# RWKV-7 chunk products on quarters of the TensorE array: 64x64 matmuls, four tiles in step

## The reference, cut to what matters

```python
def step(S, xs):
    w_t, kk_t, a_t, k_t, v_t, r_t = xs
    sa = jnp.einsum('bhvk,bhk->bhv', S, kk_t)
    S = S * w_t[:, :, None, :] - sa[..., None] * (kk_t * a_t)[:, :, None, :] + v_t[..., None] * k_t[:, :, None, :]
    y = None if r_t is None else jnp.einsum('bhvk,bhk->bhv', S, r_t)
    return S, y
```

## Time and profile before

| | |
|---|---|
| time, median of 3 runs | 4595.56 us (4587.01 to 4595.78) |
| span of the profiled execution | 4593.0 us |
| PE busy | 4060.8 us, 88% |
| DVE busy | 1998.8 us, 44% |
| POOL busy | 1020.3 us, 22% |
| ACT busy | 601.3 us, 13% |
| DMA | 211.99 MB, mean 46 GB/s |

### The profile page before, as it was taken

One profiled execution on the slowest core, in us unless ns is written; L12 is line 12 of the kernel. 1 busy time (PEld: TensorE's weight loads), 2 busy tenths in 40 slices (PEclk: granted clock), 3 DMA queues, 4 the chain that ended last, 5 costly groups with the idle time before them and its releaser, 6 DMA issues. The chain is left out here.

```text
span 4593.0 us, 57174 instructions
## 1 busy us (share of the span) xinstructions
PE 4060.8 (88%) x24068; PEld 3313.3 (72%) x24068; DVE 1998.8 (44%) x2650; ACT 601.3 (13%) x802; POOL 1020.3 (22%) x530
## 2 busy tenths in 40 slices
PE   9888879999999969977879879879869887999999
PEld 1374667888888858866858758758858866788777
DVE  0214144333433441243366566566666634434434
ACT  0211021011000020022220020020020002010010
POOL 0220232222232233211011011011011034343332
PEclk9899979999999979987979979979979987999999
DMA  8402101111011002211010010010010021111111
GB/s 314 191 19 93 37 24 36 35 40 37 28 42 37 28 28 84 74 47 40 9 40 1 6 40 1 6 40 1 4 42 1 4 78 43 42 51 46 43 53 60
DMA packets 46501, 211.99 MB, mean 46 GB/s; under 512 B 5952, under 2 KB 6976, under 8 KB 41920
## 3 DMA queue, kind: packets, MB, share of 16 engines
q1 hardware_dynamic: 42240, 191.94, 11.8%
q10 hardware_dynamic: 4032, 16.65, 0.9%
HBM read 187.73 MB, written 20.84 MB: 45 GB/s over the span
## 5 line engine op out<-in xcount | busy, mean ns | idle before, releaser
L173 PE MATMUL ps<-u_hi,w_hi 128*128 128x512 f32 (+1 forms) x2712 | 738.7, 372 | 85.8 <-DVE u_lo L404 40.8
L173 PE MATMUL ps<-u_lo,w_hi 128*128 128x512 f32 (+1 forms) x2712 | 735.7, 371 | 0.0
L173 PE MATMUL ps<-u_hi,w_lo 128*128 128x512 f32 (+1 forms) x2712 | 734.4, 370 | 0.0
L151 POOL TENSOR_TENSOR w_hi<-w_raw,zero 128x1024 fp32r<-128x1024 f32 x176 | 338.0, 1920 | 1643.1 <-PE ps L173 1430.2
L173 PEld LDWEIGHTS ps<-u_hi,w_hi 128*128 128x128 f32 x2712 | 473.7, 190 | 181.3 <-DVE u_lo L404 41.9
L173 PEld LDWEIGHTS ps<-u_lo,w_hi 128*128 128x128 f32 x2712 | 474.4, 189 | 90.3
L173 PEld LDWEIGHTS ps<-u_hi,w_lo 128*128 128x128 f32 x2712 | 473.9, 189 | 90.3
L491 DVE SCALAR_TENSOR_TENSOR ffn_cv<-ps,small,ffn_cv 128x1023 f32<-128x1023 f32 (+1 forms) x132 | 134.1, 1016 | 804.4 <-ACT ffn_cv L625 802.8
L433 DVE SCALAR_TENSOR_TENSOR h<-ps,mod,h 128x1024 f32<-128x1024 f32 (+1 forms) x288 | 282.7, 1013 | 412.8 <-PE ps L173 412.8
L154 POOL TENSOR_TENSOR w_lo<-w_raw,w_hi 128x1024 fp32r<-128x1024 f32 x176 | 425.3, 2417 | 13.8
L1743 DVE TENSOR_TENSOR rwc_x<-rwc_x,ps 128x512 f32<-128x512 f32 x360 | 247.8, 688 | 95.8 <-PE ps L1678 95.8
(11 more groups left out here) (267 smaller groups left out, 5194.7 us busy)
## 6 DMA issues: line engine op xcount, KB each, us to landing
w_raw<-in_ffn SPq DMA_DIRECT2D x132, 512.0 KB, 3.2
ada_ring<-in_ada SPq DMA_DIRECT2D x24, 2048.0 KB, 8.3
w_raw<-in_cd_in SPq DMA_DIRECT2D x20, 512.0 KB, 3.7
z_scratch<-cd_stage ACTq DMA_DIRECT2D x15, 640.0 KB, 5.1
dft_tab<-in_dft_tok SPq DMA_DIRECT2D x8, 1024.0 KB, 4.9
h<-in_x SPq DMA_DIRECT2D x8, 640.0 KB, 12.9
w_raw<-in_ab_in SPq DMA_DIRECT2D x8, 512.0 KB, 3.7
w_raw<-in_ab_out SPq DMA_DIRECT2D x8, 512.0 KB, 3.6
```

What stands on the lines that cost most here:

```text
L151: pool.tensor_tensor(K.whi[:, slot, :], K.raw[:, raw, :], K.zero[:, 0:1].to_broadcast([P, KT * P]), ALU.add).then_inc(self.hi_done, 1)
L173: mm = pe.matmul(K.ps[:, slot, c, 0:width], wt[:, s, w], x[:, k, at:at + width], start=start and n == 0, stop=stop and n == 2)
```

## The change

The two chunks of a tile are stacked on partitions, chunk 0 on 0 to 63 and chunk 1 on 64 to 127, and a unit's matrix becomes two 64x64 ones beside each other's rows: tiles M, X, XT, PX have 64 columns a unit where they had 128. Each 128x128 matmul of the levels becomes two 64x64 ones, chunk 0 on the first diagonal quarter of the array and chunk 1 on the second. In the pair, crossed and output products head and chunk choose row and column half, so that all four quarters are used in turn.

The identity is now in every plane of `R.level`, and POOL adds it to M too. M and X then carry it, so that X is not added to but replaced: DVE copies X, ACT copies XT (before, DVE added both), and DVE masks PX. The transposed start (XT) is made by POOL in two operations as before, half as wide; a third adds the identity to M, and DVE's first X waits for it (`eyed`). The two masks of stages 1 and 2 become one DVE operation over two banks, and the two copies into `rwc_tm` one.

Four tiles instead of two are in work (`NS = 4`), each with two PSUM banks, and each stage is gone through for all four before the next: groups of 4, 4 and 2 tiles. Each kind of hand-over has its own semaphores. The mask and level tables shrink to half, and so do their loads in `rwkv_prepare`.

The diff, without the removed lines of `rwkv_chunks` (they stand above) and without what only renames; the output products of Q and Y go by `both` as those of G and HP do:

```diff
-        self.mask = keep("mask", [P, 2, 2, P])
-        self.level = keep("level", [P, 6, 2, P])
+        self.mask = keep("mask", [P, 2, 2, CL])
+        self.level = keep("level", [P, 6, 2, CL])
...
+    NS = 4
...
+    SS = temp("ss", [P, NS, 2, 2, 2, 2, CL])
+    M = temp("m", [P, NS, 4, CL])
+    X = temp("x", [P, NS, 4, CL])
+    XT = temp("xt", [P, NS, 4, CL])
+    PX = temp("px", [P, NS, 4, CL])
...
+    both = [(c, hp) for hp in range(2) for c in range(2)]
+    HALF = [slice(0, 64), slice(64, 128)]
...
+    def bank(s, b):
+        return K.ps[:, s // 2, 2 * (s % 2) + b, :]
...
+    STAGES = 3 + 2 * LV + 2
+    steps = [(n, t, t % NS, t // NS) for first in range(0, TOK, NS) for n in range(STAGES)
+             for t in range(first, min(first + NS, TOK))]
         @block.gpsimd
+            for n, t, s, turn in steps:
+                if n == 2:
+                    pool.wait_ge(masked[s], turn + 1)
+                    if turn:
+                        pool.wait_ge(sq_done[s], LV * turn)
+                    xt = units(XT[:, s])
+                    pool.tensor_tensor(xt, SS[:, s, :, 0, :, 0, :], over_heads(R.level[:, 0, :, :]),
+                                       ALU.mult).then_inc(half_t[s], 1)
+                    pool.wait_ge(half_t[s], turn + 1)
+                    pool.tensor_tensor(XT[:, s], XT[:, s], K.eye2[:, :].rearrange("p (o c) -> p o c", o=1)
+                                       .to_broadcast([P, 4, CL]), ALU.add).then_inc(xt0_out[s], 1)
+                    pool.wait_ge(m_out[s], turn + 1)
+                    pool.tensor_tensor(M[:, s], M[:, s], K.eye2[:, :].rearrange("p (o c) -> p o c", o=1)
+                                       .to_broadcast([P, 4, CL]), ALU.add).then_inc(eyed[s], 1)
...
+                elif n == 1:
+                    pe.wait_ge(tm_out[s], turn + 1)
+                    for kind, src in enumerate((R.beta, R.kappa)):
+                        for d in range(2):
+                            for c, hp in both:
+                                at = kind * 256 + d * P
+                                mm = pe.matmul(bank(s, hp)[HALF[c], at:at + P], src[HALF[hp], d, toks(t, c)],
+                                               R.ar[HALF[hp], d, t, :, HALF[c]], start=True, stop=True)
+                    mm.then_inc(pairs[s], 1)
+                elif n == 2:
+                    pe.wait_ge(masked[s], turn + 1)
+                    for d in range(2):
+                        for c, hp in both:
+                            mm = pe.matmul(bank(s, hp)[HALF[c], d * CL:(d + 1) * CL], R.ar[HALF[hp], d, t, 0, HALF[c]],
+                                           R.beta[HALF[hp], d, toks(t, c)], start=True, stop=True)
+                    mm.then_inc(crossed[s], 1)
+                elif n < 3 + 2 * LV and n % 2 == 1:
+                    j = (n - 3) // 2
+                    if j == 0:
+                        pe.wait_ge(eyed[s], turn + 1)
+                        pe.wait_ge(xt0_out[s], turn + 1)
...
+                    for u in range(4):
+                        for c in range(2):
+                            mm = pe.matmul(b0[HALF[c], u * CL:(u + 1) * CL], M[HALF[c], s, u, :], XT[HALF[c], s, u, :],
+                                           start=True, stop=True)
...
+                elif n < 3 + 2 * LV:
...
+                    for u in range(4):
+                        for c in range(2):
+                            mm = pe.matmul(b1[HALF[c], u * CL:(u + 1) * CL], X[HALF[c], s, u, :], PX[HALF[c], s, u, :],
+                                           start=True, stop=True)
+                    if j < LV - 1:
+                        for u in range(4):
+                            for c in range(2):
+                                mm = pe.matmul(b0[HALF[c], 256 + u * CL:256 + (u + 1) * CL], PX[HALF[c], s, u, :],
+                                               X[HALF[c], s, u, :], start=True, stop=True)
...
+                    for d in range(2):
+                        for c, hp in both:
+                            mm = pe.matmul(bank(s, c)[HALF[hp], d * P:d * P + 64], TW[HALF[c], s, 2 * hp + d, 0:64],
+                                           TM[HALF[c], s, d, HALF[hp]], start=True, stop=True)
+                        for c, hp in both:
+                            pe.matmul(bank(s, c)[HALF[hp], d * P + 64:(d + 1) * P], TM[HALF[c], s, 2 + d, HALF[hp]],
+                                      TM[HALF[c], s, 4, HALF[hp]], start=True, stop=False)
+                        for c, hp in both:
+                            mm = pe.matmul(bank(s, c)[HALF[hp], d * P + 64:(d + 1) * P], TM[HALF[c], s, d, HALF[hp]],
+                                           TW[HALF[c], s, 2 * hp + d, 64:128], start=False, stop=True)
...
+                elif 3 <= n < 3 + 2 * LV:
+                    j = (n - 4) // 2
+                    act.wait_ge(sq_done[s], LV * turn + j + 1)
+                    act.copy(XT[:, s, :, :].rearrange("p u c -> p (u c)"), b1[:, 0:256]).then_inc(xt_out[s], 1)
...
         @block.vector
+            for n, t, s, turn in steps:
+                b0, b1 = bank(s, 0), bank(s, 1)
+                if n == 1:
+                    dve.wait_ge(pairs[s], turn + 1)
+                    dve.tensor_tensor(SS[:, s].rearrange("p h k d m c -> p (h k) (d m c)"),
+                                      banks(s).rearrange("p b (k c) -> p (b k) c", k=2),
+                                      R.mask[:, :, :, :].rearrange("p (o d) m c -> p o (d m c)", o=1)
+                                      .to_broadcast([P, 4, 256]), ALU.mult).then_inc(masked[s], 1)
+                elif n == 2:
+                    dve.wait_ge(crossed[s], turn + 1)
+                    dve.tensor_tensor(units(M[:, s]), banks(s)[:, :, 0:P].rearrange("p h (d c) -> p h d c", d=2),
+                                      over_heads(R.mask[:, ::-1, 0, :]), ALU.mult).then_inc(m_out[s], 1)
+                    dve.wait_ge(eyed[s], turn + 1)
+                    dve.tensor_tensor(units(X[:, s]), units(M[:, s]), over_heads(R.level[:, 0, ::-1, :]),
+                                      ALU.mult).then_inc(x0_out[s], 1)
+                elif 3 <= n < 3 + 2 * LV and n % 2 == 1:
+                    j = (n - 3) // 2
+                    dve.wait_ge(p_done[s], LV * turn + j + 1)
+                    dve.tensor_tensor(units(PX[:, s]), b0[:, 0:256].rearrange("p (h d c) -> p h d c", h=2, d=2),
+                                      over_heads(R.level[:, 1 + j, :, :]), ALU.mult).then_inc(p_out[s], 1)
+                elif 3 <= n < 3 + 2 * (LV - 1):
+                    j = (n - 4) // 2
+                    dve.wait_ge(sq_done[s], LV * turn + j + 1)
+                    dve.tensor_copy(X[:, s, :, :].rearrange("p u c -> p (u c)"), b0[:, 256:512]).then_inc(x_out[s], 1)
...
-    ch, sub = d // CL, np.arange(P)
-    mask = np.zeros((P, 2, 2, P), np.float32)
-    level = np.zeros((P, 6, 2, P), np.float32)
-    src, dst = sub[:, None], sub[None, :]
-    same = (src // CL) == (dst // CL)
+    src, dst = (np.arange(P) % CL)[:, None], np.arange(CL)[None, :]
+    mask = np.zeros((P, 2, 2, CL), np.float32)
+    level = np.zeros((P, 6, 2, CL), np.float32)
     for way in range(2):
         before = src < dst if way == 0 else src > dst
-        mask[:, way, 0] = same & before
-        mask[:, way, 1] = same & (before | (src == dst))
+        mask[:, way, 0] = before
+        mask[:, way, 1] = before | (src == dst)
         for i in range(6):
             b = 1 << i
             near = (src // (2 * b)) == (dst // (2 * b))
-            level[:, i, way] = near & ((src // b) != (dst // b)) & before
+            level[:, i, way] = (near & ((src // b) != (dst // b)) & before) | (src == dst)
     arr["rw_mask"], arr["rw_level"] = mask, level
```

More of the change, by code:

```diff
@@ L1761, in rwkv_chunks @@
-    on_act = lambda n, t: n in (0, M_STAGE, TW_STAGE) or (n == OUT_STAGE and t < SEQ // P)
-    on_dve = lambda n, t: n in (1, 2, M_STAGE, OUT_STAGE) or LEVEL0 <= n < TW_STAGE
-    groups, n = [], 0
-    while n < STAGES:
-        size = 2 if n == 1 or (LEVEL0 <= n < TW_STAGE - 1 and (n - LEVEL0) % 3 == 1) else 1
-        groups.append(range(n, n + size))
-        n += size
-    steps = [(n, t, s) for pair in range(TOK // 2) for group in groups
-             for s, t in ((0, 2 * pair), (1, 2 * pair + 1)) for n in group]
@@ L1772, in before @@
-    def before(n, t, s):
-        past = [(m, u) for m, u, q in steps if q == s]
-        past = past[:past.index((n, t))]
-        return sum(on_act(*x) for x in past), sum(on_dve(*x) for x in past)
-    def runs_ahead(n):
-        return n == 2 or LEVEL0 < n < TW_STAGE and (n - LEVEL0) % 3 in (0, 2)
+    NS = 4
+    TM = temp("tm", [P, NS, 5, P])
+    AZ = temp("az", [P, NS, 4, P])
+    SS = temp("ss", [P, NS, 2, 2, 2, 2, CL])
+    M = temp("m", [P, NS, 4, CL])
+    X = temp("x", [P, NS, 4, CL])
@@ new lines, in rwkv_chunks, with sems @@
+    XT = temp("xt", [P, NS, 4, CL])
+    PX = temp("px", [P, NS, 4, CL])
+    TW = temp("tw", [P, NS, 4, P])
+    LV = 5
```

(26 more changed lines are left out.)

249 lines of the change are left out of this document (86 added, 163 removed).

## The result

The changed kernel takes **4149.72 us** (median of 4 runs, 4145.81 to 4152.66) against 4591.51 us of the kernel before in the same session (4587.01 to 4595.78).

What follows compares the result with a forecast made beforehand. TensorE was taken as the bound. A chunk pass of 155 us plus 7.5 for clock and 5 for waits made 167.5 against 254.5, saving 348 us over four passes: 4248 us forecast, range 4165 to 4400.

Steps and rivals of the forecast that it cites:

- A step of 8 diagonal matmuls is thus 0.48 us: Level steps: 16 records as 8 pairs, two at once, take 0.48 us where the full-array step takes 0.89.
- levels 25.0 us: Levels of a group of four tiles, at TensorE's pace: 3.84 + 3 x 5.76 + 3.84 = 25.0 us.
- start of a group 20.5: Prologue of four tiles: GpSimd's three operations a tile delay the first squaring to 20.5 us, 4.5 us of it a stall.
- a level of two tiles 3.7: Last group, two tiles: waits are no longer covered, so a level takes 3.7 us against TensorE's 2.88.
- I take 1.78, since these rows show two at once: Pair products of a tile (stage 1): 1.78 us with two quarters at once; 0.89 if all four ran at once.
- the 48 pairs of the outputs, 2.88 us: Output stage of a latent tile: 48 matmuls counted as 48 pairs, 2.88 us of TensorE's time.
- The clock term: Sparse group starts: 3.4 to 6.9 us at half speed lose 1.7 to 3.4 us per group, 7.5 a pass.
- The wait term: About 100 steps with a wait in a pass: 15 us if each cost 0.15; 5 us taken.
- My low end: Whole kernel, 4186 us: four quarters at once in pair products, no wait cost, 4 us of clock, 152 a pass.
- Feeding the quarters: Rival: TensorE can't start records faster than the scan's 0.09 us a pair; 219 us a pass, 4455 us; chance 0.08.
- The clock at 0.5 throughout: Rival: quarter pairs fill half the array and don't keep the clock up; 278 us a pass, 4690 us; chance 0.06.
- Pairs that don't overlap: Rival: quarter matmuls take turns, so all but the transposes doubles; 271 us a pass, 4660 us; chance 0.04.

Runs made afterwards that it cites:

- numbers 1 and 2: Against the changed kernel: pair, crossed and output products reordered so neighbours alternate between two quarters, 4158.60 us; some output products issued again (G twice, Q three times), 4193.57 us.
- number 10: Changed kernel with the tiles of a pass starting one stage apart and groups running into each other, instead of four tiles together: 4097.98 us, ratio 0.8919.

## Where the prediction was right and where it was wrong

**The bound and the kind of gain**: right. TensorE was the bound and quarter products bring a level of four tiles down to the time of two. "A step of 8 diagonal matmuls is thus 0.48 us" measured 0.467; levels 25.0 us, measured 24.3; start of a group 20.5, measured 19.7; a level of two tiles 3.7, measured 3.16.

**The steps that failed** are two. The first is "I take 1.78, since these rows show two at once", and with it the 48 pairs of the outputs, 2.88 us. The scan of the earlier trace rows has products on two quarters only, so it could not show more, and I made its count the chip's. With four at once pair products take 0.88 and outputs 1.40 us. The pair products gave little of that, because GpSimd sets the end of the start. TW and outputs of a group of four took 12.8 and 12.3 us where I had 15.1; without the pauses they would be 9.8 and 9.3. The last group took 29.1 us where I had 34, 2.6 of the difference in the levels, 1.4 in the outputs and the end. With the smaller differences in the starts and levels of the other groups these terms make 13.4 us of the first pass (155.2 forecast, 141.8 measured).

**The second, as large, are the two allowances on top.** The clock term, "1.7 to 3.4 us lost" per group, 7.5 a pass, was added in full to a stage whose pace GpSimd sets: the clock did fall, for 3.4 and 6.8 us in the first two groups' starts, and for most of that TensorE still waited. Some 0.8 us was lost in the second group's start of the first pass and 0.6 in the last's (2471.20 to 2472.76, the two steps that took 0.99 at full clock). In the later passes the low clock reached the levels, 5.8 us over three passes. The wait term of 5 us has nothing in the waits of the levels: in groups of four a step came every 0.467 us, waits and all. Together the allowances were 12.5 us a pass, 50 in all; against them stand 8 us by which the three later passes were longer than the first. My low end kept 4 us of clock and two quarters in the outputs, which is why 4150 lay below it.

**What I did not see** works the other way: the pauses for instructions, 25 us. The earlier trace rows and the diff held what was needed for a warning (7,000 records more in fewer microseconds), but no row of before shows such a pause (the "issue" of 0.78 us in the earlier trace rows is another thing: it comes again at the same product of every pair of tiles, 924 records apart).

**The rivals.** Feeding the quarters: records start at 0.029 us in the levels without a ceiling, so not that; the ceiling lies at the instructions' supply, at twice that density. The clock at 0.5 throughout: the levels of the first pass ran at 1.00, and the worst stretch of levels above at 0.89. Pairs that don't overlap: single file would be 0.9 us a step. The Trainium skill (TensorEngine Tiling (Array Packing), Gotcha 1: PSUM Pressure) has different row tiles unable to access one PSUM bank at the same time; the level steps write both row tiles into one bank at 0.467 us for 16 records, so for these products, which write different partitions of the bank, the measurement decides against that sentence.

X0 on VectorE, which I put at 0.5 us, took 0.93 beside a GpSimd operation and 0.42 with none. The Trainium skill (SBUF — State Buffer, Who interferes with whom) says that a VectorE instruction with two SBUF inputs contends with a GpSimd instruction that reads SBUF; the trace agrees: of the 40 X0 of the changed kernel the 28 that overlap a GpSimd operation took 0.93 us each, the 12 others 0.42 to 0.43. In the kernel one stage apart none of the 40 overlaps one, and this line's record has 0.43 us as its most (duration least/median/most):

```profile
L1814 DVE TENSOR_TENSOR rwc_x<-rwc_m,rw_level x40: 424/426/427, 2359.8 to 3120.9; 128x256 f32<-128x256 f32 x40
```

Open stays how the queue that feeds TensorE is filled. That a pause stands every 256 instructions where the list is dense enough, and goes where it is half as dense, is shown (numbers 1 and 2); what sets the 3.2 to 4.2 us between packets, and why a pause ends 2.2 and 2.8 us after a packet's start (2401.51 after 2399.3, 2405.25 after 2402.5), isn't. Nor was a run made that holds the clock apart from the order, so the 16 us of busy time in number 10 are read from the profile only.

## What to carry to other kernels

A row that shows two things at once in work that offers two is a lower bound, not a limit: price the wider case from both ends and let the range reach to the far one. Add an allowance (clock, waits) only for the stretch in which the engine it slows sets the pace. When several tiles share the steps of a chain, try them one step apart rather than abreast (52 us here), so that one's start and end lie under another's products; but never put a step right behind the one that must first empty its place.

## What the runs showed of the hardware

- Fp32 products of 64 columns on four quarters start at 7.3 ns per instruction, weight loads counted (192 in 1.40 us); on two at 14.6 ns.
- At that density TensorE's instructions run out: pauses of 1.35 to 1.65 us with "issue" as releaser, one after every 256 instructions, 3.47 us apart when the dense stretch goes on. The instruction queue q8 brings one packet of 16 KB for 257 to 260 of TensorE's records.
- Products of a quarter overlap with those of the other even when eight records of one stand before eight of the other: 0.57 us for 16 against 0.467 when they alternate. Where the other quarters' products stood 48 records further back they didn't: 2.61 us a tile's outputs against 1.40.
- The granted clock fell to 0.50 (1.2 GHz) after 3.3 us in which TensorE was busy for 1.61, and came back to 1.00 after 3.4 us with 3.04 busy; in the second group it stayed at 0.50 for 6.8 us with 5.92 busy.
- A VectorE operation with two SBUF inputs of 128x256 took 0.93 us where it overlapped a GpSimd operation that reads SBUF and 0.42 where it didn't (28 and 12 records).
